# A conditioned two-layer decoder trunk in fp32: the modulation matrix of the first feed-forward part read in pieces of 128 rows by 1024 columns

## What is computed

```python
cond = silu(c)                                   # 2048
for l in range(2):
    mod = cond @ w_mod[l] + b_mod[l]             # 2048 x 12288 per layer
    sh1, sc1, g1, sh2, sc2, g2 = split(mod, 6)
    x = x + g1 * mixer(rms_norm(x) * (1 + sc1) + sh1)
    h = rms_norm(x) * (1 + sc2) + sh2
    u = h @ w_up[l]                              # 2048 x 11264
    a, g = split(conv3(u), 2)
    x = x + g2 * ((silu(g) * a) @ w_down[l])     # 5632 x 2048
```

## Time and profile before

| what | value |
|---|---|
| median of 3 runs | 2075.19 us (2074.86 to 2075.71) |
| profiled execution, its own time | 2075.73 us |
| profiled execution, span | 2074.1 us |
| TensorE / VectorE / ScalarE / POOL busy | 97% / 80% / 51% / 15% |
| mean granted TensorE clock | 0.993 |
| read from HBM | 554 MB, 268 GB/s over the span |

### The profile page before, as it was taken

The page is one execution under the profiler, slowest core; times in us unless marked ns, Lnnn a source line. Parts: engine busy times, 40 slices in busy tenths (PEclk is TensorE's granted clock), DMA queues, the critical chain, the costliest instruction groups (busy, mean ns, idle before and its releaser), DMA issues.

```text
span 2074.1 us, 33153 instructions
## 1 busy us (share of the span) xinstructions
PE 2004.5 (97%) x12242; PEld 1790.8 (86%) x12242; DVE 1655.3 (80%) x2321; ACT 1054.6 (51%) x1551; POOL 309.0 (15%) x459
## 2 busy tenths in 40 slices
PE   3999999999999999999999999899999999999998
PEld 3888989888999889999899987688888888888886
DVE  5786899887899998998988986898965666666665
ACT  4323774544554544565445555555543555434553
POOL 3242342220121122112212110011100000000000
PEclk9999999999999999999999999999999999999999
DMA  9999899885789899888998884397765555555552
GB/s 360 355 368 328 302 330 332 296 303 202 272 314 327 323 354 346 323 300 309 357 355 290 320 297 142 98 332 270 255 203 190 195 183 186 200 184 194 191 184 100
DMA packets 235851, 558.39 MB, mean 269 GB/s; under 512 B 14024, under 2 KB 15032, under 8 KB 235192
## 3 DMA queue, kind: packets, MB, share of 16 engines
q1 hardware_dynamic: 180408, 355.03, 49.6%
q0 software_dynamic: 55296, 201.35, 27.1%
HBM read 554.23 MB, written 2.10 MB: 268 GB/s over the span
## 4 chain that ended last, share of the span: by engine, by line
PE 88%; DVE 5%; ACT 2%; issue 2%; DMA 2%; POOL 0%; DVEq 0%; ACTq 0%; POOLq 0%
PE ps L677 15%; PE ps L702 10%; PE ps L704 10%; PE ps L703 10%; PE ps L655 9%; PE ps L657 9%; PE ps L656 9%; PE ps L682 8%; PE ps L722 3%; DVE w_lo L1520 1%; PE ps L719 1%; DVE macc L1534 1%; DMA early<-in_w_mod 1%; ACT work L1106 1%; DMA mraw<-in_w_mod 1%
## 5 line engine op out<-in xcount | busy, mean ns | idle before, releaser
L1106 ACT ACTIVATE w_hi<-raw 128x1024 fp32r<-128x1024 f32 x640 | 668.0, 1056 | 729.5 <-PE ps L704 242.3
L1520 DVE TENSOR_TENSOR w_lo<-raw,w_hi 128x1024 fp32r<-128x1024 f32 x640 | 766.3, 1225 | 291.4 <-ACT w_hi L1106 290.4
L655 PE MATMUL ps<-h_pair,w_hi 128*128 128x256 f32 x1792 | 512.6, 286 | 2.7 <-DVE w_lo L1520 2.3
L657 PE MATMUL ps<-h_pair,w_lo 128*128 128x256 f32 x1792 | 507.4, 283 | 0.0
L656 PE MATMUL ps<-h_pair,w_hi 128*128 128x256 f32 x1792 | 507.3, 283 | 0.0
L1534 DVE SCALAR_TENSOR_TENSOR macc<-mraw,cond,macc 128x512 f32<-128x512 f32 x620 | 428.0, 749 | 54.8 <-DMA mraw<-in_w_mod 46.7
L540 POOL DMA_DIRECT2D mraw<-in_w_mod x358 | 258.7, 723 | 1167.7 <-DVE macc L1534 870.1
L677 PE MATMUL ps<-h_pair,w_hi 128*128 128x512 f32 x1408 | 354.9, 394 | 1.4 <-DVE w_lo L1520 1.3
L655 PEld LDWEIGHTS ps<-h_pair,w_hi 128*128 128x128 f32 x1792 | 344.2, 192 | 5.5 <-issue 5.4
L656 PEld LDWEIGHTS ps<-h_pair,w_hi 128*128 128x128 f32 x1792 | 344.2, 192 | 1.3 <-issue 1.1
L657 PEld LDWEIGHTS ps<-h_pair,w_lo 128*128 128x128 f32 x1792 | 344.0, 192 | 0.0
(11 more groups left out here) (177 smaller groups left out, 1512.2 us busy)
## 6 DMA issues: line engine op xcount, KB each, us to landing
mraw<-in_w_mod POOLq DMA_DIRECT2D x358, 512.0 KB, 6.4
raw<-in_w_up SPq DMA_DIRECT2D x176, 1024.0 KB, 6.5
raw<-in_w_down SPq DMA_DIRECT2D x88, 1024.0 KB, 5.8
raw<-in_w_attn_in SPq DMA_DIRECT2D x48, 1024.0 KB, 8.5
raw<-in_w_attn_out SPq DMA_DIRECT2D x16, 1024.0 KB, 7.3
work<-in_w_mod POOLq DMA_DIRECT2D x12, 512.0 KB, 8.7
early<-in_w_mod POOLq DMA_DIRECT2D x8, 512.0 KB, 12.9
raw<-in_w_pool SPq DMA_DIRECT2D x4, 1024.0 KB, 5.3
```

What stands on the lines that cost most here:

```text
L655: mm(o, wh, ah, start=st, stop=False, skip_group_check=True)
L657: i = mm(o, wl, ah, start=False, stop=last_half and kk == 1, skip_group_check=True)
L1106: return nc.scalar.activation(o, i, f, **kw)
L1520: V.tensor_tensor(w_lo[:, s, :, :], raw[:, j % 4, h * 1024:(h + 1) * 1024].rearrange("p (k n) -> p k n", k=2), w_hi[:, s, :, :].bitcast(F3 ...
```

## The change

The chunks 20 to 43 are taken in twelve pairs. A pair is read in sixteen pieces of 128 rows by 1024 columns, again 512 KB each, into the same four buffers: buffer p % 4, issued when piece p-4 has been used. In SBUF a piece is now 128 partitions by one row of 1024. Piece 0 is one instruction on ScalarE (`pair_start`), pieces 1 to 15 are one instruction each on VectorE (`pair_step`), all into one accumulator of 1024 columns, and each waits for the one before it. The addition of two accumulators is gone in this part. Both chunks of a pair are summed after the pair's last piece, the first at least two steps later and the second two steps after the first. The chunks before 20 and from 44 on stay as they were; `since` corrects their semaphore counts. `WORK` is `[0.0] + [1.33] * 15` per pair, and the steps of all pieces and sums come out anew.

```diff
-        WORK = ([0.0] + [1.33] * 6 + [2.2]) * (44 - CH_MLP)
+        WORK = ([0.0] + [1.33] * 15) * ((44 - CH_MLP) // 2)
...
-                MLP_AT[u].append((CH_MLP + n // 8, n % 8))
-                if n % 8 == 7:
-                    MLP_SUM[max([u + 2] + [v + 1 for v in MLP_SUM])] = CH_MLP + n // 8
+                MLP_AT[u].append((n // 16, n % 16))
+                if n % 16 == 15:
+                    for odd in range(2):
+                        MLP_SUM[max([u + 2] + [v + 2 for v in MLP_SUM])] = CH_MLP + n // 16 * 2 + odd
...
+            def pair_piece(l, i, c_l, p):
+                if p >= 4:
+                    if p == 4:
+                        pool.wait_ge(pair_first, i + 1)
+                    else:
+                        pool.wait_ge(pair_acc, 15 * i + (p - 4))
+                elif isinstance(i, int) and i == 0:
+                    pool.wait_ge(mod_acc, 14 * CH_MLP + 2 * p - 6)
+                else:
+                    pool.wait_ge(pair_acc, 15 * i + (p - 3))
+                pool.dma_start(pair_slot(p), w_mod[l, P * p:P * p + P, ds(512 * c_l, 1024)]
+                               ).then_inc(mod_landed[p % 4], 16)
...
+            def pair_start(i):
+                act.wait_ge(*pair_landing(i, 0))
+                act.wait_ge(mod_red, max(CH_MLP + 2 * i - 2, CH_MLP - 1))
+                A(pair_whole(i), pair_slot(0), ACT.Copy, scale=cond[:, 0:1]).then_inc(pair_first, 1)
...
+            def pair_step(i, p):
+                if p:
+                    dve.wait_ge(*pair_landing(i, p))
+                    if p == 1:
+                        dve.wait_ge(pair_first, i + 1)
+                    else:
+                        dve.wait_ge(pair_acc, 15 * i + p - 1)
+                    V.scalar_tensor_tensor(pair_whole(i), pair_slot(p), cond[:, p:p + 1], pair_whole(i),
+                                           ALU.mult, ALU.add).then_inc(pair_acc, 1)
```

More of the change, by code:

```diff
@@ L407, in decoder_trunk, with pair_rows, pair_whole, pair_slot @@
                 n = 8 * (44 - CH_MLP) - len(WORK) - 1
-                MLP_AT[u].append((CH_MLP + n // 8, n % 8))
-                if n % 8 == 7:
-                    MLP_SUM[max([u + 2] + [v + 1 for v in MLP_SUM])] = CH_MLP + n // 8
+                MLP_AT[u].append((n // 16, n % 16))
+                if n % 16 == 15:
+                    for odd in range(2):
+                        MLP_SUM[max([u + 2] + [v + 2 for v in MLP_SUM])] = CH_MLP + n // 16 * 2 + odd
         assert len(WORK) == 0 and max(MLP_SUM) < len(STEPS)
+        PAIRS = (44 - CH_MLP) // 2
+        def pair_rows(c):
+            return macc[:, ((c - CH_MLP) // 2 + 1) % 2, (c - CH_MLP) % 2, :]
+        def pair_whole(i):
+            return macc[:, (i + 1) % 2].rearrange("p k n -> p (k n)")
+        def pair_slot(p):
+            return mraw[:, p % 4].rearrange("p k n -> p (k n)")
+        def pair_landing(i, p):
+            return mod_landing(CH_MLP + 2 * i + p // 8, p % 8)
+        def since(c_all):
+            return c_all - 2 * PAIRS if isinstance(c_all, int) and c_all >= 44 else c_all
         def mlp_step(quad, j):
@@ L568, in pieces, with late_piece @@
                         piece(l, i + l * CHUNKS, i, j)
+            def pair_piece(l, i, c_l, p):
[10 more added lines that the diff above has]
+                               ).then_inc(mod_landed[p % 4], 16)
+            def late_piece(c_l, j):
+                n = c_l + CHUNKS - 2 * PAIRS
+                if j >= 4:
+                    if j == 4:
+                        pool.wait_ge(mod_first, 2 * n + 2)
+                    else:
+                        pool.wait_ge(mod_acc, 14 * n + 2 * j - 8)
+                elif n == CH_MLP:
+                    pool.wait_ge(pair_acc, 15 * PAIRS + j - 3)
+                else:
+                    pool.wait_ge(mod_acc, 14 * n + 2 * j - 6)
+                land(1, c_l, j, mraw[:, j % 4], mod_landed[j % 4])
             def first_piece(c_all, j):
@@ L634, in _ @@
             assert steps[0] == C_POOL
-            pieces(0, 13, CHUNKS)
-            pieces(1, 0, CHUNKS)
+            pieces(0, 13, CH_MLP)
+            for i in range(2):
+                for p in range(16):
+                    pair_piece(0, i, CH_MLP + 2 * i, p)
+            with pool.Fori(2, PAIRS) as i:
+                for p in range(16):
+                    pair_piece(1, i, 2 * i - 4, p)
+            for c_l in range(20, CHUNKS):
+                for j in range(8):
+                    late_piece(c_l, j)
         @block.tensor
@@ L742, in mod_sum, with mod_flip, pair_gate_sum @@
                 i.then_inc(mod_red, 1)
-            def mod_flip(c_all, a):
-                pe.wait_ge(mod_added, c_all + 1)
+            def mod_flip(c_all):
+                pe.wait_ge(pair_acc, 15 * ((c_all - CH_MLP) // 2 + 1))
                 pe.wait_ge(mod_ready, c_all)
                 for t in range(4):
-                    i = nc.tensor.transpose(ps[:, 7, t * P:(t + 1) * P], macc[:, a, 0, t * P:(t + 1) * P], ident[:, :])
+                    i = nc.tensor.transpose(ps[:, 7, t * P:(t + 1) * P], pair_rows(c_all)[:, t * P:(t + 1) * P],
+                                            ident[:, :])
                 i.then_inc(mod_red, 1)
+            def pair_gate_sum(c_all):
+                pe.wait_ge(pair_acc, 15 * ((c_all - CH_MLP) // 2 + 1))
+                pe.wait_ge(mod_ready, c_all)
+                mm(ps[:, gate_bank(c_all), :], ones[:, :], pair_rows(c_all),
+                   start=True, stop=True).then_inc(mod_red, 1)
             def gate_sum(c_all, a):
-                pe.wait_ge(mod_added, c_all + 1)
+                pe.wait_ge(mod_added, since(c_all) + 1)
                 pe.wait_ge(mod_ready, c_all)
@@ L1353, in chunk_first @@
                 def chunk_first(quad, j):
-                    for c, p in MLP_AT[mlp_step(quad, j)]:
+                    for i, p in MLP_AT[mlp_step(quad, j)]:
                         if p == 0:
-                            first_products(c, (c + 1) % 2, c - 1)
+                            pair_start(i)
                 def chunk_columns(quad, j):
@@ L1530, in piece @@
                         if j == 1:
[L1531 removed]
+                            dve.wait_ge(mod_first, 2 * since(c_all) + kk + 1)
                         else:
[L1533 removed]
+                            dve.wait_ge(mod_acc, 14 * since(c_all) + k - 3)
                         V.scalar_tensor_tensor(macc[:, a, kk, :], mod_slot(c_all, j)[:, kk, :], cond[:, k:k + 1],
@@ L1825, in chunk_pieces @@
                 def chunk_pieces(quad, j):
-                    for c, p in MLP_AT[mlp_step(quad, j)]:
-                        piece(c, p, (c + 1) % 2)
+                    for i, p in MLP_AT[mlp_step(quad, j)]:
+                        pair_step(i, p)
                 def chunk_bias(quad, j):
```

9 lines of the change are left out of this document (6 added, 3 removed).

## The result

| | before | after |
|---|---|---|
| median of 6 runs, same chip | 2075.24 us | 2152.36 us (2151.09 to 2159.49) |
| ratio, 95% interval | | 1.0375 [1.0364, 1.0385] |
| profiled execution, its span | 2075.73, 2074.1 us | 2151.32, 2149.7 us |

The change costs 77 us. The forecast was 2072.2 with a range up to 2075.8: the time lies 80 us above the forecast and 77 us above the end of the range, on the side to which I had given 0.09.

What follows compares the result with a forecast made beforehand. TensorE was taken to bound the kernel, with only its 6.2 us of waiting for VectorE's late w_lo to win. The terms summed to -3.0 us, from 2075.73 to 2072.7, or 2072.2 as a median; range 2069.2 to 2075.8.

Steps and rivals of the forecast that it cites:

- the side to which I had given 0.09: The outcome that the changed kernel is measurably slower, over 2079.3 us; chance 0.09.
- The burst is the new bound: Rival: transfers of 4 KB rows land later and stall seven unit starts, +7.5 us at 1.5 us more; chance 0.09.
- Price of a piece: On VectorE, one piece of 1024 columns takes 1.28 us, bounded by 1.222 and 1.50.
- Waiting for the piece before: On VectorE, each piece directly behind another costs 0.13 us: 0.04 between them and 0.09 of lost overlap, in about 95 cases.
- Unit 80: At this unit's start VectorE finishes its pieces 3.3 us earlier and TensorE's stall goes, -1.56 us.
- Unit 24: At this unit's start a buffer comes free later and TensorE arrives earlier, so it gets worse, +1.5 us (0.5 to 2.5).
- Unit 64: At this unit's start, the same shape as unit 24, but its lead should just cover the delay.
- given back: Rival: other handoffs between pairs behave like unit 24 at two or three places, +3, time stays at 2075.2; chance 0.08.
- Unit 104: At this unit's start no column sums stand ahead on ScalarE and the last piece comes earlier, -1.5 us.
- Unit 122: At this unit's start column sums and a piece are gone, the table load stays, ScalarE is earlier, -1.2 us.
- Small ones: At units 102 and 118, two pieces instead of three behind column sums, -0.5 us.
- The crumbs: At steps 8, 32, 72 and 112, behind eight-step ends, one piece where there was none, +0.3 us together.

Runs made afterwards that it cites:

- run 6: The changed kernel with the two sums of a pair three steps apart instead of two; 2077.0 us, ratio 1.0008 to before.
- run 1: The changed kernel with the two sums of a pair four steps apart instead of two; 2077.06 us, ratio 1.0004 to before.
- Run 4: The changed kernel with a PSUM bank of its own for each pair's second sum, which waits only for the bias before last, except chunk 23; 2083.69 us.
- Run 3: The changed kernel with the sums four steps apart in every first, third, fifth pair and so on, two apart in the others; 2111.48 us.
- 7: The changed kernel with sums four steps apart and a fixed table of at most two pieces a step; 2071.47 us, ratio 0.9976 to before.
- 8: The kernel before with a fixed table of at most two pieces a step, its sums following by its old rule; 2070.33 us, ratio 0.9976.

## Why the prediction was wrong

**The step that failed** is in its first part: "the same 132 units, the same 4 gate sums and 20 sets of four transposes. What can be won is the time in which TensorE stands still because VectorE is late with `w_lo`, and nothing else." The sums are the same in number, not in place. The change has a line that moves them, `v + 1` to `v + 2` with both sums of a pair due at once. I used the table that it makes for the column sums at units 104 and 122 and for the gate sum at unit 24, and never asked what a moved sum waits for. Each has a wait on `mod_ready`, a term that the sum did not have at all. It costs nothing at four steps, 2.1 us in all at three, and 57.5 us at two.

**It could have been read from the trace of before.** Its timeline, TensorE at the start of unit 106 and VectorE in step 105, the step after the sum in step 104:

```profile
1119.18 0.28 PE L655 MATMUL ps<-h_pair,w_hi 128*128 128x256 f32 x1
...
1119.30 2.73 DVE L1534 SCALAR_TENSOR_TENSOR macc<-mraw,cond,macc 128x512 f32<-128x512 f32 x4
1121.95 2.35 DVE L1520 TENSOR_TENSOR w_lo<-raw,w_hi 128x1024 fp32r<-128x1024 f32 x2
1124.22 0.16 DVE L1836 TENSOR_TENSOR mods<-colsum,prm 128x4 f32<-128x4 f32 x1
```

The bias starts at 1124.22, 5.04 us after unit 106 has started; there nobody asks for it. A sum put in step 106 would have waited about 5 us, and 4.99 is what it waited. Unit 107 starts one unit of 5.76 us later, at 1124.94: a sum there finds the bias done at 1124.38. So two steps cost 5 us here and three cost nothing, close to what the changed kernel and run 6 found. Twelve times 5 is 60, against 57.5 measured. That this is so near is in part luck, since the twelve waits run from 2.57 to 7.1 us. The clock's 18 us don't show in the rows of this part, where TensorE is never idle that long. But the trace of before has one such case just behind it: TensorE waits 5.21 us until 1319.10. Two windows of it, with the columns as above:

```profile
1314.00:1319.00 5.00, 0.00 (x0) 0.00 (x0) 3.85 (x9) 3.05 (x10) 0.00 (x0) 0.85 0.00 0
1319.00:1322.00 3.00, 2.90 (x14) 2.93 (x15) 1.67 (x4) 1.27 (x3) 0.00 (x0) 0.50 0.00 0
```

The granted clock is at half for the next three microseconds, which would have pointed at more than the waits themselves. The sum would have been some +60 and more, not −3.0.

**The rivals.** None held. "The burst is the new bound" had the right sign for another reason; landings took 6.0 us (median) in the changed kernel and 6.3 in run 1, not 7.9.

**The terms.** The changed kernel's stalls cover them, so they are read from three runs without most of the stalls. Run 4 has the pieces and the sums where the changed kernel has them, and one stall, at unit 26. Runs 1 and 6 have the same pieces, but the second sum of each pair is two steps or one later. The times from the start of the unit before to the start of this one, from the timelines, in us:

| unit | before | run 4 | run 6 | run 1 |
|---|---|---|---|---|
| 24 | 6.29 | 8.25 | 8.18 | 8.46 |
| 36 | 5.80 | 6.15 | 5.81 | 6.72 |
| 64 | 6.37 | 7.65 | 6.12 | 8.37 |
| 104 | 8.15 | 6.93 | 6.90 | 7.88 |
| 122 | 7.00 | 6.12 | 6.18 | 7.02 |

- *Price of a piece*: 1.28 forecast, 1282 ns measured.
- *Waiting for the piece before*: two in a row take 2.67 us, so 0.11 between them, not 0.04. With the overlap of 0.09 lost, a wait costs 0.20 us, not 0.13. The section of the Trainium skill that the prediction cites (VectorE: DVE Perf Modes, section "The DRAIN you can't avoid") found that a semaphore cost nothing extra, on eight copies. For the pieces here the trace does not agree: 0.20 us each. VectorE was relieved by 14.7 us in the whole kernel instead of 21 in this part.
- *Unit 80*: −1.56 forecast; in run 1 units 78 to 80 take 12.02 us instead of 13.59, −1.57; the stall is gone. Right.
- *Unit 24*: +1.5 forecast; in run 1 units 23 to 25 take 14.29 instead of 12.36, +1.9, and in runs 4 and 6 it is +1.7 and +1.6. Right in kind, a little small.
- *Unit 64*: "their leads should just cover it", 0. It takes 1.3 us more in run 4 and 2.0 more in run 1. The same handoff as unit 24, shown above: piece 0 of the next pair is awaited on ScalarE for 8.32 us, and `w_hi` stands behind it. The rival "given back" named such places; it had the mechanism. In run 6, where TensorE has lost 0.7 us around unit 58, unit 64 loses nothing: these stalls hang together.
- *Unit 104*: −1.5 forecast; −1.2 in runs 4 and 6, near it. In run 1 it is −0.3 only: a sum stands in step 99 again and its column sums are back on ScalarE ahead of the taps. Run 3 has a sum there too, and takes 7.77 us.
- *Unit 122*: −1.2 forecast; −0.9 in run 4 and −0.8 in run 6, near it. In before and in runs 1, 3, 7 and 8 a sum stands in step 119, and in all five the unit takes 7.0 us. In all runs without a sum there it takes 6.11 to 6.18. The column sums are worth 0.9 us at this place. The table load stands there in both, and no run moved it. TensorE's wait at the start of unit 122, before and in run 4:

```profile
1213.93 0.47 PE L702 MATMUL ps<-w_hi,g_hi 128*128 128x512 f32 x1 [1.40 <-DVE w_lo L1520]
...
1222.95 0.47 PE L758 MATMUL ps<-w_hi,g_hi 128*128 128x512 f32 x1 [0.52 <-DVE w_lo L1591]
```

- *Unit 36*, no term: +0.9 in run 1, +0.35 in run 4, 0 in run 6.
- *Small ones*: −0.5 forecast at 102 and 118; −0.3 each in run 1. Right. The crumbs: +0.4 at unit 55 in run 1, not at the steps that I had named.

From the first unit's start to the last one's, before takes 763.3 us, run 1 takes 766.2 (+2.9) and run 6 takes 762.8 (−0.4, with 2.1 us of waits for a bias in it). Run 4 takes 770.7, of which the one stall is about 6.5, so some +1. I had −3.0. So apart from the waits for a bias the forecast was out by some 0.5 us in run 6, 4 us in run 4 and 6 us in run 1 (2 of these for the column sums that are back), most of it at units 64 and 24. What the pieces themselves are worth is not settled more closely than that. (Run 1 enters the part 2.0 us earlier, which nothing in the change explains; its ratio, 1.0004 [0.9995, 1.0013], is −1 to +2.7 us.)

Of the things I had named that would show it right or wrong, the sum of TensorE's waits over 5 us was the one that spoke.

## What to carry to other kernels

A change of a table or a rule of order moves every instruction that hangs on it. For each moved one list its waits, find in the trace of before when the awaited instruction ends and where the waiting one will now start, and subtract; here two rows give 5 us for one place of the twelve. A side result that stands last in an engine's step is late: here VectorE's step 105 runs beside TensorE's unit 106, so the bias is ready only when TensorE should be nearly through that unit. And before making an operation cheaper, see whether its inputs arrive evenly: the same pieces, at most two a step, won 5 us, and wider ones nothing that could be measured.

## What the runs showed of the hardware

- The stall of 4.99 us cost about 6.5: behind it the granted clock is 0.50 for two microseconds and 0.90 for the next two, and TensorE's busy time in the whole kernel grows (2027.8 us against 2004.5) with the same matmuls. Of two waits of 2.57 us one was followed by half clock and one was not.
- A transfer of 128 rows of 4 KB is issued by POOL in 529 ns, one of 256 rows of 2 KB in 723 ns; the landing is 6.0 us in the slower changed kernel and 6.3 in run 1, against 6.4. In 192 transfers that freed POOL of 37 us that nobody waited for.
- ScalarE's copy of 1024 columns from `mraw` took 1144 ns when it wrote `macc`, 1057 when it wrote `w_hi`; I had priced the one by the other. At twelve of them it doesn't matter.
